# Gate and up products in seven block products per pair, with the weight sums formed by adding transfers

## The reference

```python
h = rmsnorm(x, g_mix)
qa, ka, va, qb, kb, vb, rb, a1, ga, gb = split(h @ w_in)      # 1024 x 6672
oa = sliding_window_attention(rmsnorm(qa), rmsnorm(ka), va)   # 16 query heads, 4 key heads, sinks, ALiBi
ob, state = gated_linear_attention(qb, kb, vb, decay(a1 @ w_a2 + b_a))   # 4 heads
m = sigmoid(ga) * oa + sigmoid(gb) * rmsnorm(ob) * silu(rb)
x = x + m @ w_out
f = rmsnorm(x, g_ffn)
y = x + (silu(f @ w_gate) * (f @ w_up)) @ w_down              # w_gate, w_up: 1024 x 2816
```

## Time and profile before

| | |
|---|---|
| median of 3 runs | 966.62 us (965.98 to 967.33) |
| profiled execution | 966.65 us, its span 964.8 us, TensorE clock granted 0.996 |
| TensorE busy | 927.0 us, 96% |
| VectorE, ScalarE, GpSimd busy | 43%, 36%, 34% |
| loads | 71.87 MB read from HBM, 3.60 MB written |

### The profile page before, as it was taken

One profiled execution on the slowest core, in us unless ns is written; L12 is line 12 of the kernel. 1 busy time (PEld: TensorE's weight loads), 2 busy tenths in 40 slices (PEclk: granted clock), 3 DMA queues, 4 the chain that ended last, 5 costly groups with the idle time before them and its releaser, 6 DMA issues.

```text
span 964.8 us, 17928 instructions
## 1 busy us (share of the span) xinstructions
PE 927.0 (96%) x7315; PEld 885.9 (92%) x7315; DVE 413.6 (43%) x850; ACT 350.0 (36%) x641; POOL 327.6 (34%) x139
## 2 busy tenths in 40 slices
PE   3999999999887999999999999999999999999997
PEld 3889999988887989888899999999999999999997
DVE  5682646566776445656543353331123331123311
ACT  5552433433444544454543442221122221122231
POOL 2442313121222222323233344444334444334450
PEclk9999999999998999999999999999999999999999
DMA  8332222212322122122152223222233222232212
GB/s 236 89 87 67 57 69 63 65 56 57 96 66 66 46 66 66 46 67 57 55 158 72 83 83 93 87 87 88 87 88 87 87 87 88 87 89 76 65 56 70
DMA packets 140786, 77.03 MB, mean 80 GB/s; under 512 B 2832, under 2 KB 139494, under 8 KB 140726
## 3 DMA queue, kind: packets, MB, share of 16 engines
q1 hardware_dynamic: 134262, 71.88, 26.2%
q10 hardware_dynamic: 6464, 4.29, 1.7%
HBM read 71.87 MB, written 3.60 MB: 78 GB/s over the span
## 4 chain that ended last, share of the span: by engine, by line
PE 80%; DVE 12%; ACT 5%; issue 2%; DMA 1%; ACTq 1%; SPq 0%; DVEq 0%
PE G L489 23%; PE G L491 22%; PE G L490 22%; PE X L655 2%; DVE qAT L1326 2%; PE X L639 1%; ACT prob L976 1%; PE X L626 1%; DVE prob L1352 1%; DVE rs L1129 1%; DVE rs L1128 1%; DVE rt L1130 1%; PE X L582 1%; ACT rs L902 1%; DVE rv L1291 1%
## 5 line engine op out<-in xcount | busy, mean ns | idle before, releaser
L467 POOL TENSOR_TENSOR w_lo<-wraw,w_hi 128x1024 fp32r<-128x1024 f32 x129 | 325.9, 2526 | 613.1 <-ACT w_hi L815 612.9
L489 PE MATMUL G<-h_hi,w_hi 128*128 128x272 f32 x1280 | 384.4, 300 | 11.4 <-DVE rv L1291 9.1
L491 PE MATMUL G<-h_hi,w_lo 128*128 128x272 f32 x1280 | 371.3, 290 | 0.0
L490 PE MATMUL G<-h_lo,w_hi 128*128 128x272 f32 x1280 | 369.4, 289 | 0.0
L489 PEld LDWEIGHTS G<-h_hi,w_hi 128*128 128x128 f32 x1280 | 242.1, 189 | 23.1 <-issue 20.2
L490 PEld LDWEIGHTS G<-h_lo,w_hi 128*128 128x128 f32 x1280 | 242.7, 190 | 0.5
L491 PEld LDWEIGHTS G<-h_hi,w_lo 128*128 128x128 f32 x1280 | 241.9, 189 | 0.0
L489 PE MATMUL G<-f_hi,w_hi 128*128 128x272 f32 x704 | 203.0, 288 | 0.0
L491 PE MATMUL G<-f_hi,w_lo 128*128 128x272 f32 x704 | 202.9, 288 | 0.0
L490 PE MATMUL G<-f_lo,w_hi 128*128 128x272 f32 x704 | 202.1, 287 | 0.0
L815 ACT ACTIVATE w_hi<-wraw 128x1024 fp32r<-128x1024 f32 x129 | 135.3, 1049 | 89.1 <-PE G L491 89.1
(11 more groups left out here) (223 smaller groups left out, 930.9 us busy)
## 6 DMA issues: line engine op xcount, KB each, us to landing
wraw<-in_w_in_dram SPq DMA_DIRECT2D x53, 512.0 KB
wraw<-in_w_gate_dram SPq DMA_DIRECT2D x22, 512.0 KB
wraw<-in_w_up_dram SPq DMA_DIRECT2D x22, 512.0 KB
wraw<-in_w_down_dram SPq DMA_DIRECT2D x16, 512.0 KB
xtok<-in_x_prompt_dram SPq DMA_DIRECT2D x8, 512.0 KB, 4.9
wraw<-in_w_out_dram SPq DMA_DIRECT2D x8, 512.0 KB
wraw<-in_w_down_dram SPq DMA_DIRECT2D x8, 384.0 KB
out_dram<-ytok ACTq DMA_DIRECT2D x8, 256.0 KB, 2.3
```

The lines of the kernel that those rows point to most:

```text
L467: pool.tensor_tensor(w_lo[:, slot, :, :], wraw[:, slot, :, :], w_hi[:, slot, :, :].bitcast(F32), ALU.subtract).then_inc(w_split, 1)
L489: pe.matmul(o, w_hi[:, slot, kc, :], b_hi[:, kc, cols], start=(kc == 0), stop=False)
L490: pe.matmul(o, w_hi[:, slot, kc, :], b_lo[:, kc, cols], start=False, stop=False)
L491: mm = pe.matmul(o, w_lo[:, slot, kc, :], b_hi[:, kc, cols], start=False, stop=(kc == last))
```

## The change

A pair's four block products, two outputs (gate, up) by two halves of the tokens over two halves of the features, are eight products of 4 blocks each before. They become seven, by the form of Strassen's scheme that needs four sums of weights and four sums of activations. In each, TensorE takes 4 blocks x 3 matmuls of 272 columns.

- The sums of weights (up1 + up2; that minus gate1; up1 minus gate1; and the second minus gate2) are formed from negated copies that ScalarE writes (`negatives`, `last_negative`) and by four DMAs per pair that GpSimd issues with an adding write, of 256 KB each, two from HBM and two inside SBUF.
- The sums of activations (`ffn_input`) are formed by VectorE while the output projection runs. For the last four feature blocks five numbers per token pair are rounded and subtracted instead of two.
- In gate and up VectorE writes all low parts: three of 128 x 1024 and one of 128 x 512 per pair, where GpSimd wrote two of 128 x 1024. For the other tiles GpSimd still does.
- Partial products are added on their way out of PSUM by seven VectorE instructions and one ScalarE copy of 272 columns; two pairs' banks alternate (G and X). Three products add onto a bank that was read, and wait for that.
- The residual is loaded by columns (`xcol`) during the output projection. The norm factor of up and down is applied when a down tile is read out: two VectorE instructions per tile instead of one.
- In the mixer ScalarE's copy carries the gain of the query and key norm, so that VectorE's last step is a plain product; `biases` moves to just behind the mean of a query tile. The score step of the linear attention issues its transposes first, then the large products, then the small ones. EARLY is 2 instead of 3.
- The feed-forward loops are written out. `w_lo`, `h_lo` and the rest keep their names.

The core of the diff:

```diff
+            def up_weights(q, n, col):
+                raw_free(sp, n)
+                src = w_up[0, :, col:col + P].rearrange("(k p) n -> p k n", p=P)
+                sp.dma_start(wraw[:, n % RING, HK:KC, :], src[:, HK:KC, :]).then_inc(wload[n % RING], 32)
+                if q >= 2:
+                    sp.wait_ge(pair_lo, 3 * (q - 1))
+                sp.dma_start(csum[q % 2][:, 0], src[:, 0:HK, :]).then_inc(in_s1[q % 2], 16)
...
+            def first_sums(q):
+                _, n = PAIRS[q]
+                pool.wait_ge(in_s1[q % 2], 16 * (q // 2 + 1))
+                add_up(csum[q % 2][:, 0], q, 1, s1_ok[q % 2])
+                pool.wait_ge(neg_ok, 2 * q + 1)
+                add_up(wraw[:, (n + 1) % RING, 0:HK, :], q, 0, s3_ok[q % 2])
+                pool.wait_ge(neg_ok, 2 * q + 2)
+                pool.wait_ge(s1_ok[q % 2], 16 * (q // 2 + 1))
+                pool.dma_start(csum[q % 2][:, 1], csum[q % 2][:, 0], accum_op=ALU.add).then_inc(s2_ok[q % 2], 16)
+            def last_sum(q):
+                pool.wait_ge(neg4_ok, q + 1)
+                pool.wait_ge(s2_ok[q % 2], 16 * (q // 2 + 1))
+                pool.dma_start(csum4[:, :, :], csum[q % 2][:, 1], accum_op=ALU.add).then_inc(s4_ok, 16)
...
+                for q in range(q0, q0 + m):
+                    if q + 1 < q0 + m:
+                        last_sum(q + 1)
+                    if q + 2 < q0 + m:
+                        first_sums(q + 2)
+                lows(range(DN0[g], DN0[g] + KC))
...
+                pe.wait_ge(pair_lo, 3 * q + 1)
+                product(b1, w_hi[:, r0, k1], w_lo[:, r0, k1], fa_hi[:, :, 0], fa_lo[:, :, 0],
+                        ready=now(0))
+                pe.wait_ge(pair_lo, 3 * q + 3)
+                product(b5, c_hi[s][:, 0], c_lo[s][:, 0], fa_hi[:, :, 1], fa_lo[:, :, 1])
...
+                product(b6, c_hi[s][:, 1], c_lo[s][:, 1], fb_hi[:, :, 3], fb_lo[:, :, 3], ready=now(HK))
+                if q == 0:
+                    x2_squares()
+                product(b7, w_hi[:, r1, k1], w_lo[:, r1, k1], fb_hi[:, :, 2], fb_lo[:, :, 2])
+                pe.wait_ge(p1_ok, q + 1)
+                product(b1, w_hi[:, r0, k2], w_lo[:, r0, k2], fb_hi[:, :, 0], fb_lo[:, :, 0], adds=True)
+                pe.wait_ge(evicted, 6 * q + 2)
+                product(b7, w_hi[:, r1, k2], w_lo[:, r1, k2], fb_hi[:, :, 4], fb_lo[:, :, 4], adds=True)
+                pe.wait_ge(evicted, 6 * q + 3)
+                pe.wait_ge(c4_lo_ok, q + 1)
+                product(b5, c4_hi, c4_lo, fb_hi[:, :, 1], fb_lo[:, :, 1], adds=True)
...
                     mean_square(ps, 1.0 / HD, (set_free[s], 1))
+                    if kind == "qA":
+                        biases(i)
...
-                    dst, g = (kAT, G_K) if kind == "kA" else (qAT, G_Q)
-                    dve.scalar_tensor_tensor(out=dst[:, i, :], in0=raw[:, s, :], scalar=param[:, g:g + 1],
-                                             in1=rt[:, :], op0=ALU.mult, op1=ALU.mult).then_inc(norm_done, 1)
+                    dst = kAT if kind == "kA" else qAT
+                    dve.tensor_tensor(dst[:, i, :], raw[:, s, :], rt[:, :], ALU.mult).then_inc(norm_done, 1)
```

More of the change, by code:

```diff
@@ L103, with gemms @@
 USES += [1] * (N_TILES - N_IN)
+PAIRS = [(g, GU0[g] + 2 * i) for g, m in enumerate(FF_GROUPS) for i in range(m)]
+FIRST = [sum(FF_GROUPS[:g]) for g in range(len(FF_GROUPS))]
+PAIR_OF = {}
+for _q, (_g, _n) in enumerate(PAIRS):
+    PAIR_OF[_n] = PAIR_OF[_n + 1] = _q
+    USES[_n] = USES[_n + 1] = 0
+HK = KC // 2
 POST_TILES = [n for n in range(N_IN) if USES[n] == 2]
+def gemms(n):
+    return sum(m not in PAIR_OF for m in range(n))
 def uses_before(n):
@@ new lines, in _ @@
+            for i in range(RING):
+                weights(OUT0 + i, w_out, 0, KC, i * P)
+            sp.wait_ge(gb_used, KC)
+            sp.wait_ge(qk_done, NU)
+            residual(0)
+            residual(1)
+            for i in range(RING, KC):
+                weights(OUT0 + i, w_out, 0, KC, i * P)
+                residual(i - 2)
+            for g, m in enumerate(FF_GROUPS):
+                for i in range(m):
+                    c = (FIRST[g] + i) * P
+                    weights(GU0[g] + 2 * i, w_gate, 0, KC, c)
+                    up_weights(FIRST[g] + i, GU0[g] + 2 * i + 1, c)
+                    if g == 0 and i < 2:
+                        residual(KC - 2 + i)
+                for i in range(KC):
+                    weights(DN0[g] + i, w_down, FIRST[g] * P, m, i * P)
@@ new lines, in product @@
+            def product(bank, a_hi, a_lo, b_hi, b_lo, adds=False, ready=None):
+                for kc in range(HK):
+                    if ready is not None:
+                        pe.wait_ge(f_ok, ready + kc + 1)
+                    pe.matmul(bank, a_hi[:, kc, :], b_hi[:, kc, :], start=(kc == 0 and not adds), stop=False,
+                              skip_group_check=adds)
+                    pe.matmul(bank, a_hi[:, kc, :], b_lo[:, kc, :], start=False, stop=False, skip_group_check=adds)
+                    mm = pe.matmul(bank, a_lo[:, kc, :], b_hi[:, kc, :], start=False,
+                                   stop=(kc == HK - 1), skip_group_check=adds)
+                mm.then_inc(prod_done, 1)
@@ new lines, in _ @@
+                for q in range(FIRST[g], FIRST[g] + m):
+                    more = q + 1 < FIRST[g] + m
+                    last_sum_low_part(q)
+                    if q > FIRST[g]:
+                        gated(q - 1)
+                    if more:
+                        low_parts(q + 1, 0)
+                    evict_6(q)
+                    if q > FIRST[g]:
+                        mid_low_part(q - 1)
+                    evict_7(q)
+                    if more:
+                        low_parts(q + 1, 1)
+                    evict_2(q)
+                    if more:
+                        low_parts(q + 1, 2)
+                    evict_4(q)
+                    evict_3(q)
@@ new lines, in _ @@
+                gated(FIRST[g] + m - 1)
+                mid_low_part(FIRST[g] + m - 1)
+                for i in range(KC):
+                    n = DN0[g] + i
+                    dve.wait_ge(gemm_done, gemms(n + 1))
+                    x = x2T[:, i, :]
+                    if g or i:
+                        dve.wait_ge(x_added, g * KC + i)
+                    dve.tensor_tensor(h2(rs[:, :]), halves(G[n % 2]), h2(rv[:, :]), ALU.mult)\
+                        .then_inc(set_free[n % 2], 1)
+                    dve.wait_ge(set_free[n % 2], uses_before(n) + 1)
+                    dve.tensor_tensor(x, x, rs[:, :], ALU.add).then_inc(x_added, 1)
+                    if i == KC - 2 and g < len(FF_GROUPS) - 1:
+                        for part in range(3):
+                            low_parts(FIRST[g + 1], part)
```

513 lines of the change are left out of this document (326 added, 187 removed).

## The result

The changed kernel takes 972.61 us (median of 5 runs, 970.76 to 974.12) against 966.34 us for the one before on the same chip: a ratio of 1.0065 with a 95% interval of 1.0049 to 1.0080. It is slower by 0.65%, where 944 us and faster was forecast. The range of 933 to 978 us holds the time, since it was wide enough for the rivals too; the forecast's own range (936 to 952 us) does not.

The account below looks back on a forecast made before the run. The prediction took TensorE as the bound (80% of the chain of waits), VectorE in the query tiles. Its terms, led by -33.1 and +11.4, summed to -22.9 us from 966.65, so 944 us; 8-in-10 range 933 to 978, forecast's own 936 to 952.

Parts of the forecast that it names:

- The landing: Gate and up: an adding transfer's time from issue to landing, L, taken as 4.0 us and hidden; 0 to +34 us.
- 2L + c: Gate and up: lower bound on a pair's period from GpSimd's queue, two landings L plus one issue c; 9.0 us assumed.
- Rival 1: Gate and up: GpSimd's queue sets the period and the kernel is slower, 978 us at L = 5.7; chance 0.20.
- The price of an adding byte: Gate and up: DMA engines busy 7.0 to 10.5 of 10.53 us per pair, taken as hidden; 0 to +62 us.
- Rival 2: Gate and up: DMA engines are full and loads come late, 962 us or, at three times the price, 1006; chance 0.15.
- The gain of 12 matmuls: Gate and up: 84 matmuls instead of 96 per pair, 1.50 us less each, -33.1 us over 22 pairs.
- Rival 3: Gate and up: VectorE sets the period, 956 us, or 962 if GpSimd's descriptor writing waits for VectorE; chance 0.10.
- The entry, +11.4: Start of gate and up: a longer chain from output tiles to the second pair, +11.4 us, between +6 and +16.
- Query tiles, -6.2: Mixer: penalties go under VectorE's idle 1.49 us, cycle 8.20 to 7.25 us, -6.2 us (0 to -9.1).
- First down tile of the last group, +1.1: Last group's first down tile waits for the last pair's `h_lo`, 4.8 us against five blocks of 0.75, +1.1 us.
- the score order: Mixer's linear attention: same matmuls reordered, one semaphore at the end, -0.8 us, between +0.5 and -3.
- The first output tile: Output projection: two early blocks instead of three, +0.6 us (0 to 1).

Follow-up runs that it names:

- e3_plain: The changed kernel with its four adding transfers per pair writing plainly, so the weight sums are not formed: 940.08 us, one run.
- e10_two: The changed kernel with negatives, GpSimd's sums and norm factor reordered, and two of four weight sums made by VectorE instead of adding transfers: 943.05 us.
- e2_bias: The kernel before with only the query tiles' penalties (`biases`) moved behind the mean: 959.79 us, ratio 0.9928.
- e1_mixer: The kernel before with only the three mixer edits (gain in ScalarE's copy, `biases` moved, score order): 953.84 us, ratio 0.9871.
- e4_quarter: The changed kernel with each adding transfer moving only the first of four feature blocks, so sums are incomplete: 936.79 us, one run.

## Why the prediction was wrong

The step that failed is the one on the transfers, in two terms that the prediction had bounded and then taken at the friendly side.

- **The landing, taken as 4.0 us between the lone row of 2.3 and the crowded one of 5.0**. Measured: 4.7 inside SBUF, 6.9 and 8.3 from HBM. By 2L + c with the two landings in series, 6.9 + 4.7 + 0.9 = 12.5 us against the measured mean period of 11.96. Rival 1 had the right mechanism and threshold (the gain gone at a period of 11.8 us), and its 20% were too few. What it missed is that the loop closes through ScalarE, whose last negative stands behind the rounding of the sum that has just landed. The reason given against the crowded rows, that they were issued in bursts, was no reason: GpSimd issues three of its four transfers within 1.5 us here as well.
- **The price of an adding byte, taken as one to two times a plain one.** It is 2.3 times, so the engines are wanted for 3.5 + 7.4 = 10.9 us by the queues' rows (10.2 to 10.5 by share times period) of a pair that was to last 10.53. Rival 2 said that twice leaves no room, and yet the forecast called "first to second" hidden. The two rivals were priced as alternatives; they are one mechanism, since busy engines are what makes a landing long, and no run shows the engines themselves as the bound. Loosening the loop brought 0.7 us of the 1.47, and taking bytes away the rest.
- **The fit.** The Trainium skill, DMA: Bandwidth & Descriptors, "Anatomy of one DMA — SWDGE (gpsimd) path", gave 2.6 us for 256 KB. The trace disagrees: 3.7 us for the plain write inside SBUF in e3_plain and 4.7 to 8.3 with the add. The row of before with 5.0 was the better guide.

What held:

- **The gain of 12 matmuls.** Forecast 10.53 us per pair; 10.49 in e3_plain and 10.52 in e10_two.
- **VectorE.** Forecast 9.64 us of a pair; 8.7 to 8.9 measured (61.16 / 7 in e3_plain, 8.87 in the pair shown). The 3.3 us for slips were not needed. Rival 3 is refuted: with 9.8 us of work (68.44 / 7) TensorE does not wait. A form of it with descriptors was not seen either: in e10_two VectorE's and GpSimd's work lie side by side in every period and it stays at 10.52.
- **The entry, +11.4.** In e3_plain, where transfers don't disturb, the output tiles take 49.21 us from the first residual addition to the last in place of 45.61. Group 1 takes 99.72 us; the 102.76 of before less eight times the 1.54 us that a pair gains (12.03 - 10.49) would be 90.4. That is 3.6 + 9.3 = 12.9. The low parts of 1360 columns take 1.58 us, where 1.57 was extrapolated from the earlier trace rows. The slower clock was not in the sum. In the changed kernel the entry costs more, 4.2 + 10.3 us against before in all of group 1, less what its periods gain.
- **Query tiles, -6.2.** -6.4 alone; cycle 7.22 us in e2_bias and 7.26 in the changed kernel, against 7.25. That the gain would not shorten the product of 2.79 us holds too: as a plain product it takes 2.83. The Trainium skill, SBUF — State Buffer, "Who interferes with whom", says that a VectorE instruction with two inputs in SBUF contends with a GpSimd instruction that reads there. The trace agrees: GpSimd's `w_lo` runs from 240.17 for 2.38 us, and the product beside it, from 240.29, takes 2.83 us, where VectorE's other products of 544 columns take 0.72.
- **First down tile of the last group, +1.1.** In e3_plain group 3 takes 69.96 us from the last down tile before it to its own first. A down tile of six blocks is 36 matmuls, 4.5 us; six pairs are 62.9 and the entry (just below) 1.3, so 1.2 us are lost; 0.90 of them stand in TensorE's timeline as a wait for `h_lo`. The tail cost 0.1 in place of 0.8 (from the last down tile's read-out to the end 6.4 us before, 6.5 after).

What the prediction left out: **the entry into groups 2 and 3**. The first product of a group goes into a PSUM buffer that the last down tile has just left, so TensorE waits until VectorE has read it. Before, two buffers took turns there. The row, from TensorE's timeline of e3_plain:

```profile
694.09 0.36 PE L856 MATMUL G<-fa_hi,w_hi 128*128 128x272 f32 x1 [1.02 <-DVE rs L1839]
```

With it group 2 takes 91.27 us, where 6.05 for a down tile and 8 x 10.49 are 89.97: 1.3 us, twice.

What else was off: **the score order**, -4.7 in place of -0.8 and outside its bound of -3, because only waits were counted and not what changing between kinds of matmul costs.

**The first output tile** was not off, though it looks so: its residual addition comes 5.1 us later than in e1_mixer, where +0.6 was taken, and 0.9 to 3.2 us later in seven kernels with the same mixer (from 499.47 in e4_quarter to 501.81 in e3_plain). Set side by side with e1_mixer, the changed kernel is 3.3 us behind at the last low part of the first norm (32.43 against 29.14): VectorE waits for the load of x until 10.54 us instead of 8.90, and TensorE's matmuls of 272 columns take 0.43 us until 27.4 instead of 22.0 us, and 0.29 after. Another 1.1 us come at 283 to 298 us, where the granted clock is 0.90, 0.50 and 0.92 in three stretches of 5 us, and 0.67, 0.99 and 1.00 in e1_mixer. What is left, 0.65 us, is the same in e3_plain and e4_quarter, and is the EARLY that was priced at 0.6. Why this one execution started late is open; the kernel before has its last low part at 30.39, so 2.0 of the 6.1 us between the two spans lie there.

The sum with measured terms, for e3_plain: -33.9 for 22 pairs, +12.9 for the entry, +1.3 for that of group 2 and +2.5 for group 3 with its first down tile, +0.1 for the tail and -9.5 up to the first residual addition make -26.6 us, and the two spans are 964.8 and 938.2. From there to the changed kernel it is 32.7 us: 29.6 in the 19 periods (13.4, 10.9 and 5.3 in the three groups), 0.7 behind the last pair of group 2, and 1.8 + 0.6 up to the last output tile. So nothing in gate and up is left over but the transfers. Why group 1 loses more than group 2 was not tested. It is neither GpSimd's long stand for the negative L977 (15.8 us, and 16.7 in e3_plain, where it costs nothing) nor the clock (0.99 over group 1's periods in both).

## What to carry to other kernels

When a change trades arithmetic for transfers, price two things before the gain: the engines' time per byte (an add costs more than twice a plain byte here), and the longest loop that goes through a landing, followed through every engine that has something else queued ahead of its step. Moving an instruction to loosen one loop can close another, as the negative at the head of ScalarE's turn did. If the nearest rows for a landing lie on both sides of the threshold, the one taken in traffic is the one to use. A small sum that VectorE has the time to make (0.68 us) is cheaper than a transfer that costs GpSimd 0.86 us and all sixteen engines 1.5 us.
